# Four value units as one fp32 product each, the search for the row numbers ahead of the second tile's, and the row numbers turned inside a unit

## The reference, cut to what matters

```
q, k, v, qi, ki, wi = split(rmsnorm(x, g) @ w_in)      # 1024 x 3396 weights, fp32
q, k, qi, ki = rope(...)
score = sum_h relu(qi_h . ki) * wi_h * scale, causal
idx   = top_k(score, 64)                               # per query
out   = softmax(q . k[idx]) @ v[idx]                   # 8 heads of 128
```

## Time and profile before

| | us |
|---|---|
| median of 3 runs | 639.33 (638.12 to 642.69) |
| profiled execution | 640.23 |
| its span | 638.4 |

### The profile page before, as it was taken

The page is one execution under the profiler, slowest core; times in us unless marked ns, Lnnn a source line. Parts: engine busy times, 40 slices in busy tenths (PEclk is TensorE's granted clock), DMA queues, the critical chain, the costliest instruction groups (busy, mean ns, idle before and its releaser), DMA issues.

```text
span 638.4 us, 12887 instructions
## 1 busy us (share of the span) xinstructions
PE 594.6 (93%) x5106; PEld 511.8 (80%) x5106; DVE 462.7 (72%) x848; ACT 364.6 (57%) x613; POOL 242.1 (38%) x259
## 2 busy tenths in 40 slices
PE   6999745987999999999999989998999999999996
PEld 6888643886888888888888878886888888888885
DVE  4689969535588777778768786688877777785532
ACT  6676433645477555666565668655666665563322
POOL 3232146651325444454010199923255554420000
PEclk9999977988999999999999999999899999999998
DMA  9785397322857666668998864016566666778601
GB/s 262 206 216 132 102 270 225 100 67 74 276 183 215 196 194 196 195 196 247 253 278 222 238 170 121 1 50 181 168 197 199 199 196 194 214 218 237 174 6 69
DMA packets 205638, 113.85 MB, mean 178 GB/s; under 512 B 5586, under 2 KB 202306, under 8 KB 205554
## 3 DMA queue, kind: packets, MB, share of 16 engines
q1 hardware_dynamic: 203385, 106.89, 59.4%
q0 software_dynamic: 1680, 5.79, 2.6%
q10 hardware_dynamic: 512, 0.35, 0.2%
HBM read 109.36 MB, written 3.90 MB: 177 GB/s over the span
## 4 chain that ended last, share of the span: by engine, by line
PE 64%; DVE 19%; DMA 5%; ACT 5%; issue 4%; POOL 2%; DVEq 0%; SPq 0%; ACTq 0%; POOLq 0%
PE acc L1367 18%; PE acc L1373 18%; PE acc L1370 18%; DVE w_lo L896 6%; ACT w_hi L565 2%; DMA stage<-in_w_ffn_down 2%; DMA area<-in_cache_k,gix 1%; PE acc L1481 1%; PE acc L1483 1%; PE acc L1482 1%; DVE area L1026 1%; DMA stage<-in_w_rec_in 1%; PE misc L1673 1%; DVE aL L905 1%; DMA area<-in_x_prompt 1%
## 5 line engine op out<-in xcount | busy, mean ns | idle before, releaser
L1367 PE MATMUL acc<-aH,w_hi 128*128 128x264 f16 (+1 forms) x936 | 260.8, 279 | 2.3 <-DVE aL L905 2.0
L1370 PE MATMUL acc<-aL,w_hi 128*128 128x264 f16 (+1 forms) x936 | 260.4, 278 | 0.0
L1373 PE MATMUL acc<-aH,w_lo 128*128 128x264 f16 (+1 forms) x936 | 260.3, 278 | 0.0
L896 DVE SCALAR_TENSOR_TENSOR w_lo<-stage,w_hi 128x1024 f16<-128x1024 f32 (+1 forms) x159 | 208.1, 1312 | 42.5 <-ACT w_hi L565 42.4
L565 ACT ACTIVATE w_hi<-stage 128x1024 f16<-128x1024 f32 (+1 forms) x159 | 175.8, 1108 | 44.5 <-PE acc L1373 27.5
L1367 PEld LDWEIGHTS acc<-aH,w_hi 128*128 128x128 f16 (+1 forms) x936 | 92.6, 99 | 18.2 <-DVE aL L905 2.5
L1367 PE MATMUL acc<-zH,w_hi 128*128 128x264 f16 x384 | 106.0, 276 | 0.0
L1370 PE MATMUL acc<-zL,w_hi 128*128 128x264 f16 x384 | 106.0, 276 | 0.0
L1373 PE MATMUL acc<-zH,w_lo 128*128 128x264 f16 x384 | 106.0, 276 | 0.0
L1370 PEld LDWEIGHTS acc<-aL,w_hi 128*128 128x128 f16 (+1 forms) x936 | 94.0, 100 | 14.9 <-issue 0.3
L1373 PEld LDWEIGHTS acc<-aH,w_lo 128*128 128x128 f16 (+1 forms) x936 | 93.9, 100 | 14.2
(11 more groups left out here) (398 smaller groups left out, 943.8 us busy)
## 6 DMA issues: line engine op xcount, KB each, us to landing
stage<-in_w_ffn_up SPq DMA_DIRECT2D x88, 512.0 KB, 4.1
stage<-in_w_ffn_down SPq DMA_DIRECT2D x32, 704.0 KB, 5.9
stage<-in_w_attn_in SPq DMA_DIRECT2D x26, 512.0 KB, 5.5
stage<-in_w_rec_in SPq DMA_DIRECT2D x16, 512.0 KB, 5.2
stage<-in_w_attn_out SPq DMA_DIRECT2D x8, 512.0 KB, 3.8
stage<-in_w_rec_out SPq DMA_DIRECT2D x8, 512.0 KB, 3.8
area<-in_x_prompt SPq DMA_DIRECT2D x2, 512.0 KB, 5.0
out_new_k_prompt<-area SPq DMA_DIRECT2D x2, 512.0 KB, 8.6
```

The source lines that it names most:

```text
L896: v.scalar_tensor_tensor(low, stage[:, place_in_line(u) % 4, 0:n, 0:cols], WSCALE, high, ALU.mult, ALU.subtract).then_inc(lo_done, 1)
L1367: t_.matmul(out, high[:, c, :], xH[:, x0 + c, :], start=first and c == 0, stop=False)
L1370: t_.matmul(out, high[:, c, :], xL[:, x0 + c, :], start=False, stop=False)
L1373: ins = t_.matmul(out, low[:, c, :], xH[:, x0 + c, :], start=False, stop=last and c == n - 1)
```

## The change

1. `DIRECT` names units 13 to 16 (v2 to v5). They are not split. TensorE multiplies the fp32 weights in `stage` by an fp32 copy of the normalised input, `x32`, in eight fp32 matmuls. `x32` lies where the keys will be (`kT`), and ScalarE writes it in eight pieces in steps 4 to 11. The staging place of such a unit is free when TensorE has ended the unit (`unit_done`).
2. `SPLIT_AT` sets the steps of the other splits: up to unit 12 four steps ahead, as before; from unit 17 on three steps ahead. Steps 9 to 13 hold none.
3. The second tile is searched in steps 13 to 16, two rounds each, behind the merged search.
4. The row numbers are spread by TensorE inside unit 14 and picked out at the start of VectorE's step 14; the weights of the sample are turned inside unit 23. The queries' way through HBM stands behind load 17 on SP's queue.
5. VectorE multiplies sample keys in steps 17 to 20, behind the low half; the sample's maximum is taken at the end of step 21; `o_low` stands before `rope`; the end of the sample's softmax stands before the low half of its step.

```diff
+DIRECT = U_V[2:6]
+SPLIT_AT = {u: u - SLOTS if u < DIRECT[0] else u - SLOTS + 1 for u in range(SLOTS, U_OUT + SLOTS) if u not in DIRECT}
+def splits_until(place):
+    return place + 1 - sum(u <= place for u in DIRECT)
+def splits_of_step(step):
+    return [u for u, at in SPLIT_AT.items() if at == step]
...
+        x32 = kT
...
-                if place >= SLOTS:
-                    sp.wait_ge(lo_done, place - SLOTS + 1)
+                if place - SLOTS in DIRECT:
+                    sp.wait_ge(unit_done, place - SLOTS + 1)
+                elif place >= SLOTS:
+                    sp.wait_ge(lo_done, splits_until(place - SLOTS))
...
-                if u == 21:
+                if u == 17:
                     sp.wait_ge(smp_kept, 1)
                     sp.dma_start(q_rows, smp[:, 0, :]).then_inc(q_out, 16)
...
+                scale = 1.0 if u in DIRECT else INV
...
+                if 4 <= u < 4 + DC:
+                    c = u - 4
+                    nc.scalar.activation(x32[:, c, :], hT[:, c, :], ACT.Copy, scale=gcol[:, c:c + 1]).then_inc(x32_done, 1)
...
-                if u < U_OUT:
-                    hi(u + 4)
+                if u != 27:
+                    for x in splits_of_step(u):
+                        hi(x)
...
-                if u == 15:
+                if u == 14:
                     dve.wait_ge(phys_turned, 1)
...
+                if LG + 5 <= u:
+                    o_low(u - LG - 5)
                 if u < U_OUT and u not in U_V:
                     rope(u)
-                if LG + 5 <= u:
-                    o_low(u - LG - 5)
...
-                if u < U_OUT:
-                    lo(u + 4)
+                if 13 <= u < 17:
+                    take_second(2)
...
+                for x in splits_of_step(u):
+                    lo(x)
...
-                if u in (7, 8):
-                    take_second(2)
-                if u in (13, 14):
-                    take_second(2 if u == 13 else 1)
...
-                if 16 <= u < 20:
-                    sample_dots(u - 16)
+                if 17 <= u < 21:
+                    sample_dots(u - 17)
...
+            def unit_direct(u, between):
+                place = place_in_line(u)
+                pe.wait_ge(loaded[place % 4], 16 * (place // 4) + 16)
+                pe.wait_ge(x32_done, DC)
+                bank_free(u)
+                for c in range(DC):
+                    ins = t_.matmul(acc[:, u % 4, 0:T], stage[:, place % 4, c, :], x32[:, c, :], start=c == 0, stop=c == DC - 1)
+                    if between and c < DC - 1:
+                        between(2 * c)
+                ins.then_inc(unit_done, 1)
...
+                    elif u == 14:
+                        between = lambda i: turn_picked() if i == 8 else None
+                    elif u == 23:
+                        between = lambda i: turn_weights() if i == 8 else None
```

More of the change, by code:

```diff
@@ L343, in build @@
         acc_read = sem("acc_read")
+        x32_done = sem("x32_done")
         x_in = [sem(f"x_in{i}") for i in range(2)]
@@ L551, in _ @@
         def _(act):
-            steps = Steps(act, act_step)
             def hi(u):
@@ new lines, in _ @@
+                if u == 21:
+                    dve.wait_ge(sl_turned, 1)
+                    past = E[0:NS, :]
+                    small(v.tensor_reduce(smx[:], past.rearrange("p (s k) -> p s k", s=NS), AX.X, ALU.max))
+                    v.tensor_tensor(by_head(md[:]), heads, smx[:].unsqueeze(1).to_broadcast([NS, H, NS]), ALU.mult)
+                    v.tensor_tensor(sl[:].rearrange("p (j s r) -> p s j r", j=4, s=NS), past.rearrange("p (s j r) -> p s j r", s=NS, j=4),
+                                    smx[:].unsqueeze(2).unsqueeze(3).to_broadcast([NS, NS, 4, 16]), ALU.subtract).then_inc(smx_done, 1)
@@ L1472, in sample_values, with turn_picked, turn_weights @@
                 t_.matmul(E[:, 64 + 8 * h:72 + 8 * h], vgat[:, j, h * P:(h + 1) * P], pb[:, j, h, :], start=j == 0, stop=j == 3)
+            def turn_picked():
+                pe.wait_ge(prm_kept, 1)
+                pe.wait_ge(mask_set, 6)
+                pe.wait_ge(phys_done, 1)
+                t_.matmul(C[:, 0:P], of_sample[:], pf, start=True, stop=True).then_inc(phys_turned, 1)
+            def turn_weights():
+                pe.wait_ge(smx_done, 1)
+                t_.matmul(E[:, 192:256], ones[0:NS, :], md[:], start=True, stop=True)
+                t_.matmul(E[:, 256:264], ones[0:NS, :], seld[:], start=True, stop=True)
+                pe.wait_ge(sexp_done, 1)
+                for j in range(4):
+                    ins = t_.transpose(E[:, 8 * j:8 * j + 8], sl[:, j * P:(j + 1) * P], ident[0:NS, 0:NS])
+                ins.then_inc(sp_turned, 1)
             def chunk(u, c, xH, xL):
@@ L1511, in _ @@
                 if u < U_OUT:
-                    unit(u, aH, aL, between=(lambda i: sample_values(4 * (u - 24) + i // 4, i % 4)) if u in (24, 25) else None)
+                    if u in (24, 25):
+                        between = lambda i: sample_values(4 * (u - 24) + i // 4, i % 4)
+                    elif u == 14:
+                        between = lambda i: turn_picked() if i == 8 else None
+                    elif u == 23:
+                        between = lambda i: turn_weights() if i == 8 else None
+                    else:
+                        between = None
+                    unit(u, aH, aL, between=between)
                 if u == 4:
@@ L1581, in _ @@
                 heads_of_step(u)
-                if u == 20:
+                if u == 21:
                     pe.wait_ge(qb_read, 4)
@@ L1588, in _ @@
                     ins.then_inc(sl_turned, 1)
-                if u == 22:
-                    pe.wait_ge(smx_done, 1)
-                    t_.matmul(E[:, 192:256], ones[0:NS, :], md[:], start=True, stop=True)
-                    t_.matmul(E[:, 256:264], ones[0:NS, :], seld[:], start=True, stop=True)
-                    pe.wait_ge(sexp_done, 1)
-                    for j in range(4):
-                        ins = t_.transpose(E[:, 8 * j:8 * j + 8], sl[:, j * P:(j + 1) * P], ident[0:NS, 0:NS])
-                    ins.then_inc(sp_turned, 1)
                 if u == 25:
```

71 lines of the change are left out of this document (32 added, 39 removed).

## The result

The changed kernel takes 636.15 us at the median of 17 runs (634.13 to 639.62), the kernel before 639.93 us (17 runs, 638.12 to 644.7). The ratio is 0.9928, with a 95% interval of 0.9908 to 0.9947: 4.6 us faster (3.4 to 5.9; the medians themselves differ by 3.8), where 8.8 us were forecast. The profiled execution took 634.54 us (span 632.7), 1.6 under its own median, against 640.23 (638.4) before. So the two traces differ by 5.7 us, and single microseconds of one trace are read with that in mind.

A forecast was written before the change was run, and what follows sets the result against it. VectorE up to the row numbers, then the gather, then VectorE again were taken to set 60 to 166 us. Gains 2.7 + 0.4 + 3.9 + 1.8 = 8.8 us, and 0.9 to the median, took 640.2 to 630.5 us; range 623.5 to 637.

The forecast's parts named there:

- the front up to head 1's logits: Direct units to head 1's logits: row numbers at 69.9 us, gather 70.3, first product 90.8, logits' end 109.9.
- 2.7 us earlier: End of head 1's logits: at 109.9 instead of 112.6 us, a gain counted in full in the sum.
- standing elsewhere: VectorE, 89.26 to 112.6 us: the sample maximum (1.45 us) leaves this stretch, part of 4.2 us less work.
- The 0.4 for the turned weights: Step 22's turned weights moved into unit 23: 0.85 us off one hand-over, counted as 0.4 (ends 0 and 0.85).
- The late terms, 3.9 + 1.8: Pauses at 132.58 and 152.7 us: 3.9 us from the first with its low clock, 1.8 from the second.
- The forecast's 1.9 us for the clock behind the first pause: TensorE, 132.6 to 136.6 us: clock near 1.2 GHz behind head 0's low-half pause, 1.9 us lost.
- A (quick loads): Rival, weight loads beside the gather: VectorE never waits, first product near 84.0, 15.6 us gained, 624 us; chance 0.15.
- B: Rival: loads of 14.0 us leave only late gains, 634 us, or late pauses half removed, 635 to 637; chance 0.32.
- C (the clock stays low): Rival: pauses at 80 to 103 us keep TensorE at its lower clock through the heads, some 647 us; chance 0.08.

The follow-up runs named there:

- E5: Changed kernel with a small plain copy in place of the four gathers of the sample's keys, leaving out its key rows; 631.32 us, ratio 0.9855.
- E4: Changed kernel with the low half again behind the rotation and the sample's softmax end behind its step's low half; 641.4 us, ratio 1.0007.
- E3: Kernel before, with only the low half ahead of the rotation and the sample's softmax end ahead of step 26's low half; 633.19 us, ratio 0.9886.
- E1: Changed kernel with the sample's maximum moved ahead of the low half in VectorE's step 21; 632.62 us, ratio 0.9876.
- E9: Changed kernel with low half and softmax end back in their old order, and the maximum ahead of step 21's low half; 638.93 us, ratio 0.9982.
- E8: Kernel before with only a head's low half put ahead of the rotation; 636.94 us, ratio 0.9937.
- E2: Changed kernel without direct units: units 13 to 16 split four steps ahead as before, other moves kept; 640.26 us, ratio 1.0005.
- E6: Changed kernel with the queries' way out and back three steps later in SP's queue; 634.33 us, ratio 0.9897.
- E7: Kernel before, low half ahead of rotation, softmax end ahead of step 26's low half, second tile's search behind the merged one; 632.28 us, ratio 0.9872.
- E10: Changed kernel with the maximum ahead of step 21's low half and the queries one step later in SP's queue; 632.3 us, ratio 0.9881.

## Why the prediction was wrong

**Right: the front up to head 1's logits.** Each step of it stands in the first table above: fp32 units at 0.445 us per instruction, weight loads of 0.19 us under them, a load of 11.1 us beside the gather (10.8 taken), ScalarE's wait for it. E5 shows the cause of that wait. The lead in this trace is 2.0 where 2.7 was forecast. That it came so near is in part luck: in the other three traces with the same front the wait for load 18 was longer, and the lead 1.4, 1.0 and 0.0.

**Wrong: "2.7 us earlier", carried to the end.** This is the term that was mis-sized. Its value at the end is 0, not 2.7. From E4, all of the front without the late moves costs 0.4 us (give or take 2.0), where 3.1 of gain (2.7 + 0.4) were forecast. From the changed kernel against E3, the front on top of the late moves costs 2.7 us (give or take 2.6). I stopped the account at head 1's logits, and took 1.45 us for the maximum "standing elsewhere" as a gain for VectorE. I did not ask who waits for the maximum. That is ScalarE, whose step 22 begins with it, and behind ScalarE the next turn of TensorE. The block left the path of head 1's logits and entered the path of step 22, where it came behind a low half that itself waits 0.78 us for ScalarE. E1 and E9 put it ahead of the low half, and in the traces the lead comes through: 116.1 at step 22 against 117.97. The wait in step 22 is one of two places where the lead went; the other is the longer wait for load 18, as in E4's trace. The traces don't say how much each takes in the median.

**What the repaired front is worth.** E1 against E3 is 632.62 against 633.19 us: 0.6 us, with both intervals over 3 us wide. In the traces E1 leads E3 by 1.1 us at step 22 and by 0.9 at the last low half, and the spans are equal. So even repaired, nine microseconds of earlier gather give about one. In the kernel before VectorE stood 4.98 us at the first product, waiting for the keys. Now it does not wait for them; it comes late itself, behind ScalarE's two waits for loads that meet the gather (6.87 and 2.43 us), as the forecast said.

**The 0.4 for the turned weights** has no trial of its own. From step 22 to 23 the trace has 5.38 us after and 5.62 before, 0.24 less, inside the forecast's own ends for it.

**The late terms, 3.9 + 1.8, were right and left something out.** In the traces they are 3.85 (E8) and 1.69 (E3). The low clock behind the pause of 4.1 us, another 1.04 us (4.10 to 3.06 from step 27 to 28), was missing. The two moves gave 7.3 us (5.1 to 9.6) instead of 5.7; of the 8.4 us between the spans of E3 and before, 0.76 were there at step 21, ahead of both moves. The forecast's 1.9 us for the clock behind the first pause was 0.2 too much by its own row: 4 us at 0.58 lose 1.7. So the total came out 4.2 us too high from a front that gave nothing and a late part that gave more, two errors of opposite sign. In the profiled execution of the changed kernel this last part was not gained. It has the same pause of 2.35 us as E3 at the same place, and then another clock. TensorE and the window behind it, after and then E3:

```profile
146.51 0.33 PE L1463 MATMUL misc<-ca,scratch 128*128 128x128 f32 x1 [2.35 <-DVE zL L1046]
...
148.00:150.00 2.00, 2.00 (x11) 1.36 (x9) 1.57 (x2) 1.94 (x6) 0.07 (x1) 0.50 0.43 130
```
```profile
146.42 0.33 PE L1425 MATMUL misc<-ca,scratch 128*128 128x128 f32 x1 [2.35 <-DVE zL L1020]
...
148.00:150.00 2.00, 1.70 (x16) 1.30 (x14) 0.48 (x2) 1.91 (x4) 0.00 (x0) 1.00 0.28 84
```

The step from 27 to 28 takes 4.18 us in one and 3.06 in the other. Of the 2.7 us between the two spans, 0.1 are there at step 27, 1.1 come here, and the rest comes after 160 us; the clock over 320 to 380 is 0.97 in the one and 1.00 in the other.

**Against the rivals.** A (quick loads) is out. B is the nearest: it named a time of 634 with only the late gains left, for the reason that loads of 14 us push head 1's logits back by 0.5 us. In the changed kernel's trace that was not so; in E4's it nearly was (first product at 93.04, logits 0.03 us earlier than before). C (the clock stays low) is out: 0.84, 0.75 and 1.00 over the three stretches from 80 to 140 us, where it was to be under 0.65. The Trainium skill (TensorE: Matmul & The Clock Gate, section HAM oscillation) tells of a matmul kernel that waits some 3 to 5 us for DMA in each round and whose clock falls back each time. Here the pauses of 7.1 us (after) and 4.1 us (before) each had a low clock behind them, 0.50 and 0.60 in their windows, which agrees. Shorter pauses had one in one kernel and none in another, as that of 2.35 us above.

**What stays open.** Whether the low clock behind that 2.35 us pause belongs to the changed kernel's order. It stands in the profiles of the changed kernel, E2 and E6 (0.91 over 140 to 160), not in those of E1, E3, E5, E7 and E10 (1.00), of which E5 has the maximum late too. That such a fall can differ with the same instructions ahead of it is shown at step 14, where the kernel before and E3 are alike. TensorE's turn and the window behind it, before and then E3:

```profile
70.31 0.33 PE L1425 MATMUL misc<-ca,scratch 128*128 128x128 f32 x1 [3.82 <-ACT scratch L676]
...
70.30:72.30 2.00, 1.99 (x18) 1.76 (x19) 1.79 (x11) 2.00 (x4) 0.00 (x0) 1.00 0.80 236
```
```profile
70.50 0.47 PE L1425 MATMUL misc<-ca,scratch 128*128 128x128 f32 x1 [3.81 <-ACT scratch L676]
...
70.50:72.50 2.00, 2.00 (x9) 1.45 (x10) 1.79 (x11) 2.00 (x4) 0.00 (x0) 0.50 0.81 237
```

Nor is the forecast's 1.9 us behind head 0's pause certain in each execution: E9 has the same pause of 1.99 us as before, and 1.00 over the 4 us behind it, where before had 0.58. Against chance alone speaks the mean granted clock of every execution: its median is 0.976 over the changed kernel's 17 runs (0.973 to 0.984), and 0.98 over the six each of E1, E3 and E10. So the changed kernel does run at a somewhat lower clock than these; in which stretches, only the profiled executions tell. It also stays open where the 2.7 us between the changed kernel and E3 go, since their two traces are level up to step 27.

The best versions measured are E1, E3, E7 and E10, at 632.3 to 633.2 us, which can't be told apart. E3 is much the smallest edit: two blocks of VectorE's steps change places, and all units stay split.

## What to carry to other kernels

When a piece of work is moved off one path, follow its result, not only its cost: who consumes it, what stands in order behind the consumer on that engine, and who waits for that. A lead at a milestone is no gain until it has been followed through the next two hand-overs. And before preparing an earlier start of a large transfer, count what else wants the DMA engines then: a start 9.3 us earlier bought a first product 1.3 us later here, since the wait for the keys came back as a wait for the weight loads, in E6 and E10 for those that now stood behind.

## What the runs showed of the hardware

- **The wait for loads doesn't shrink by reordering.** ScalarE's waits for weight loads, summed over 60 to 125 us, are 9.3 us in the changed kernel, 9.5 in E1, 9.4 in E4 and E9, 8.8 in E10 and 12.2 in E6, for three positions of the queries' broadcast; taking the gather of keys away brought it to 1.2 (E5). With the old front the sum is lower and varies: 6.7, 5.0 and 1.9 us in before, E3 and E8, which are alike up to there. From 75 to 80 us, while the gather runs in the changed kernel, the 16 DMA engines are full (a share of 1.08) and move 348 GB/s; in E5 they are at 0.92 and move 195. The Trainium skill (DMA: Bandwidth & Descriptors, section Issuing engines are not separate DMA queues) says that transfers started by different engines run on the same 16 DMA engines and interleave; the trace agrees, with a 512 KB load at 11.1 us beside a gather of 8.6.
- **fp32 weights straight from the staging place.** 3.56 us for a unit of eight 264-column products, against 2.7 for 24 fp16 ones; the weight load of 0.19 us never showed. The price on TensorE was the forecast one. TensorE waits 5.0 us behind these units (the turn at 82.18), so they did not hold it up there; no run prices them alone.
- **Half clock behind a pause.** Behind pauses of 7 to 8 us TensorE ran at about half its clock, 1.2 of 2.4 GHz, for 3 to 6 us. Over 60 to 166 us the twelve traces have 27 waits of TensorE of 4.05 us or more, and all have a low clock in the 4 us behind them; of 19 waits between 1.9 and 3.9 us 10 have one and 9 have none, with no order by length (1.93 us had one, 3.82 us none). Where the clock rose again moved the turn of step 21 by 0.76 us between two kernels that are alike up to there: over the 4 us behind the wait of head 1's logits it is 0.50 before (turn at 114.07) and 0.50, then 0.69 in E3 (113.31). The windows of the changed kernel behind its pause of 7.1 us:

```profile
104.00:107.00 3.00, 2.46 (x9) 1.83 (x10) 2.20 (x8) 2.19 (x6) 1.84 (x3) 0.50 0.13 39
107.00:110.00 3.00, 3.00 (x16) 2.05 (x14) 2.93 (x5) 0.00 (x0) 1.90 (x1) 0.52 0.40 110
```
